# Attention of the first 256 queries four heads to a visit, two heads to a bank; last residual added on TensorE

## The chip, the cores and the metric

The kernel runs on one core of a Trainium2 chip. The metric is the device time of one launch in microseconds. The median of three runs of the kernel before is 459.55 us (459.14 to 460.91).

## What is computed

A decoder layer for 512 tokens of width 1024 in float32. One input projection feeds two causal token mixers, a gated recurrence (HGRN2) and a sparse attention, whose outputs are gated, projected, merged, projected once more and added to the input ahead of a layer norm. The parts that the change touches are these:

```python
def dsa_mix(q, k, v, q_idx, k_idx, w_idx, rel_bias):      # 8 heads of 64, blocks of 128 queries
        score = jnp.einsum('bth,bths->bts', wb * (IDX_HEADS ** -0.5), jax.nn.relu(dots))
        score = jnp.where(causal[None], score, -jnp.inf)
        _, idx = lax.top_k(score, topk)                   # 128 keys for each query, shared by all heads
        logits = jnp.einsum('bthd,btkhd->bhtk', qh, ks) * (HEAD_DIM_B ** -0.5)
        logits = logits + bias.transpose(0, 3, 1, 2)      # T5 bias of the distance
        p = jax.nn.softmax(logits, axis=-1)
        o = jnp.einsum('bhtk,btkhd->bthd', p.astype(vs.dtype), vs)
...
    merged = jax.nn.sigmoid(ga) * ua + jax.nn.sigmoid(gb) * ub
    y = jnp.einsum('bld,de->ble', merged, w_out)
    return layer_norm(ALPHA * x + y, ln_g, ln_b)
```

## The kernel before

**The stream.** Every large product is done in three matmuls of 512 columns on parts with a rounded high half and the rest as low half (`split_product`, L516 to L518). The weights come in 31 units of 256 columns (`UNITS`), then four of the output projection. A unit is four quarters of twelve such matmuls; a quarter has the number q = 4u + (0 to 3). Two PSUM banks take turns for the projections (`proj_bank`); bank i of unit u is filled in quarters 4u + 2i and 4u + 2i + 1, must be read by `leave_bank` and is filled again four quarters after it was begun. ScalarE rounds each unit's weights to `w_hi` (L842), and GpSimd (L1681), for units 17 to 24 VectorE (L1498), subtracts to get `w_lo`.

**Side work.** Behind each quarter TensorE runs `side(q)`, and ScalarE, VectorE and GpSimd have a `side(q)` of their own, in which the work of the same quarter stands in a fixed order. Every engine goes through its list in order and waits on semaphores; it may run ahead of or lag behind the others. Tables say what falls into which quarter.

**Attention.** The 32 items (`ITEMS`) are pairs of a block b of 128 queries and a head h: blocks 0 to 3 of heads 0 to 3 (items 0 to 15), then of heads 4 to 7 (16 to 31). An item has (b + 1) x 128 keys; keys outside the top k are not gathered but get a penalty. One item goes through these steps:

- GpSimd, `bias_and_penalty` (L1699, L1697): bias plus penalty into one of two `logit` buffers, that of item i once `logits` of item i - 2 has run.
- TensorE, `scores` (L652, L653): two matmuls into one of two banks (`log_bank`), in quarter `Q_ITEM[i]`.
- VectorE, `logits` (L1318): adds bank and buffer into `prob` (four buffers), negates, and takes the row's extreme.
- ScalarE, `softmax_exp` (L931); VectorE, `invert_sums` (L1329); ScalarE, `normalise` (L939).
- TensorE, `turn_probs` (L662): b + 1 turnings of 128 x 128 into one of two banks (`turn_bank`), two quarters after the scores.
- VectorE, `move_probs` (L1306): out of that bank into `prob_t`.
- TensorE, `attend` (L677): values times probabilities, two heads at a time, in quarter `Q_ATTEND[i]`; one quarter later VectorE gates the four heads (`gate_group`, L1340).

Items go two to a visit. Within a quarter TensorE does values, then turnings, then scores. VectorE does bank copies of the projection, `move_probs`, gating, `logits`, one round of the top k, sums, further rounds, then low parts and the steps of the recurrence. A round of the top k (L1294, L1295) takes the 8 largest of the remaining scores; the 16 rounds of the last query block are spread over quarters 38 to 48. ScalarE does bank copies, scalings of the quarter before (items 0 to 15), rounding of weights, exponentials, scalings of the same quarter (items 16 to 31), and then `forget`, the decay of the recurrence, that of the first two heads in quarters `Q_PREP[0]` to + 2 (64 to 66), of the others from `Q_PREP[1]`. Units 15 and 16 are the inputs of `forget`; `leave_bank` copies their banks to `cum` (L913).

**The end.** The output projection fills eight banks (`y_bank[half][t]`, four blocks of tokens, two halves of 512 columns), 24 matmuls each. For each, `residual` (L1546, L1548) adds ALPHA times the input (`x_res`) to the bank into `y_sb` and takes statistics. Behind the second half of a block VectorE joins them (L1653), centres (L1658), and scales (L1664), with the inverse deviation from ScalarE (L1178, L1180), and the two halves go out. Only the last block's second half has nothing of TensorE beside it.

## Time and profile before

| | us | share |
|---|---|---|
| median of 3 runs | 459.55 | |
| profiled execution | 459.29 | |
| its span | 457.5 | |
| TensorE busy | 449.4 | 98% |
| TensorE weight loads | 368.1 | 80% |
| VectorE busy | 292.3 | 64% |
| ScalarE busy | 223.1 | 49% |
| GpSimd busy | 163.3 | 36% |

The span runs from the first to the last instruction of the profiled execution; 1.8 us of its time lie around it. The granted clock of TensorE is 0.995 of its full 2.4 GHz over the span. Matmuls are pipelined: the time that a row gives for one is longer than the time by which it holds up the next, so their cost is read from start to start. VectorE's share is an average; from 46 to 137 us it is busy for nine tenths of the time and more.

### The profile page before, as it was taken

The page shows a single profiled execution, that of the slowest core. Times are in us where ns is not written, and L with a number is a line of the kernel's source. Part 1 is how long each engine was busy: PE and PEld are TensorE (multiplying, and loading weights), DVE is VectorE, ACT ScalarE, POOL GpSimd, SP SyncE. Part 2 cuts the span into 40 slices and gives each one's busy share as a digit, 9 for nine tenths or more (in the row PEclk, how much of TensorE's full clock was granted, in tenths as well). Part 3 has the DMA queues.
Part 4 walks back from the last instruction along what each step waited for, and adds up shares of the span by engine and source line. Part 5 has one row for each costly group of instructions (what it writes and reads, how often), then busy time and mean ns, then how long its engine had stood idle before and what let it go on. Part 6 is the DMA issues. An engine that isn't in the chain of part 4 may idle for free.

```text
span 457.5 us, 7667 instructions
## 1 busy us (share of the span) xinstructions
PE 449.4 (98%) x2970; PEld 368.1 (80%) x2970; DVE 292.3 (64%) x558; ACT 223.1 (49%) x378; POOL 163.3 (36%) x161
## 2 busy tenths in 40 slices
PE   9999999999999999999999999999999999999993
PEld 7778888888888788888888887887888888888882
DVE  4546589999999853346989994880643040662286
ACT  5735445253345746294877475735774415341000
POOL 0444432582259813581004000000064554984000
PEclk9999999999999999999999999999999999999998
DMA  8908122256023720204030222031044222374022
GB/s 251 304 15 293 73 82 93 92 152 217 0 93 92 186 92 1 93 1 149 36 95 1 95 93 93 1 122 66 1 123 153 93 92 93 119 257 176 0 92 92
DMA packets 17299, 47.73 MB, mean 104 GB/s; under 512 B 2504, under 2 KB 4336, under 8 KB 17264
## 3 DMA queue, kind: packets, MB, share of 16 engines
q1 hardware_dynamic: 17024, 47.05, 31.5%
q8 instruction: 23, 0.38, 0.3%
q10 hardware_dynamic: 240, 0.20, 0.1%
q14 instruction: 12, 0.10, 0.1%
HBM read 43.04 MB, written 2.11 MB: 99 GB/s over the span
## 4 chain that ended last, share of the span: by engine, by line
PE 98%; DVE 1%; DVEq 0%; issue 0%; POOL 0%; POOLq 0%
PE bank L516 27%; PE bank L517 26%; PE bank L518 26%; PE bank L677 2%; PE bank L662 2%; PE bank L713 2%; PE bank L760 2%; PE bank L653 1%; PE bank L652 1%; PE bank L804 1%; PE bank L642 1%; PE bank L641 1%; PE bank L559 1%; PE bank L560 1%; PE bank L564 1%; PE bank L746 1%
## 5 line engine op out<-in xcount | busy, mean ns | idle before, releaser
L1681 POOL TENSOR_TENSOR w_lo<-w_raw,w_hi 128x512 fp32r<-128x512 f32 x92 | 122.6, 1358 | 161.8 <-ACT w_hi L842 161.8
L516 PE MATMUL bank<-x_hi,w_hi 128*128 128x512 f32 x336 | 132.9, 396 | 0.0
L517 PE MATMUL bank<-x_lo,w_hi 128*128 128x512 f32 x336 | 131.1, 390 | 0.0
L518 PE MATMUL bank<-x_hi,w_lo 128*128 128x512 f32 x336 | 131.0, 390 | 0.0
L516 PEld LDWEIGHTS bank<-x_hi,w_hi 128*128 128x128 f32 x336 | 63.1, 188 | 13.9 <-issue 0.8
L518 PEld LDWEIGHTS bank<-x_hi,w_lo 128*128 128x128 f32 x336 | 63.1, 188 | 13.6
L517 PEld LDWEIGHTS bank<-x_lo,w_hi 128*128 128x128 f32 x336 | 63.1, 188 | 12.1
L842 ACT ACTIVATE w_hi<-w_raw 128x1024 fp32r<-128x1024 f32 (+2 forms) x67 | 66.5, 1014 | 10.1 <-PE bank L518 5.8
L931 ACT ACTIVATE prob<-prob,nmax 128x128 f32<-128x128 f32 (+3 forms) x32 | 17.7, 555 | 41.6 <-DVE nmax L1318 41.5
L1294 DVE MAX8 best<-score 128x8 f32<-128x256 f32 (+2 forms) x48 | 26.8, 559 | 1.1
L1306 DVE COPY prob_t<-bank 128x128 f32<-128x128 f32 (+3 forms) x32 | 14.3, 486 | 19.0 <-PE bank L662 18.9
L1295 DVE MATCH_REPLACE8 score<-best,score 128x256 f32<-128x256 f32 (+2 forms) x48 | 26.0, 542 | 0.0
L516 PE MATMUL bank<-w_hi,x_hi 128*128 128x512 f32 x64 | 25.3, 395 | 0.0
L518 PE MATMUL bank<-w_hi,x_lo 128*128 128x512 f32 x64 | 25.0, 390 | 0.0
L517 PE MATMUL bank<-w_lo,x_hi 128*128 128x512 f32 x64 | 24.9, 390 | 0.0
L516 PE MATMUL bank<-o_hi,w_hi 128*128 128x512 f32 x64 | 24.9, 389 | 0.0
L517 PE MATMUL bank<-o_lo,w_hi 128*128 128x512 f32 x64 | 24.9, 389 | 0.0
L518 PE MATMUL bank<-o_hi,w_lo 128*128 128x512 f32 x64 | 24.9, 389 | 0.0
L921 ACT ACTIVATE relus<-bank 128x256 f32<-128x256 f32 (+2 forms) x24 | 10.5, 489 | 21.0 <-PE bank L642 21.0
L1699 POOL TENSOR_TENSOR logit<-t,pen 128x256 f32<-128x256 f32 x24 | 17.4, 740 | 9.1 <-DVE nmax L1318 9.1
L1498 DVE TENSOR_TENSOR w_lo<-w_raw,w_hi 128x512 fp32r<-128x512 f32 x32 | 20.5, 683 | 0.0
L1284 DVE SCALAR_TENSOR_TENSOR score<-relus,w_idx,score 128x256 f32<-128x256 f32 (+2 forms) x21 | 15.7, 747 | 7.6 <-ACT relus L921 5.9
(206 smaller groups left out, 756.1 us busy)
## 6 DMA issues: line engine op xcount, KB each, us to landing
w_raw<-in_w_units SPq DMA_DIRECT2D x66, 512.0 KB, 4.7
out<-y_sb SPq DMA_DIRECT2D x8, 256.0 KB, 2.0
x_raw_hi<-in_x_t SPq DMA_DIRECT2D x4, 256.0 KB, 5.0
x_raw_lo<-in_x_t SPq DMA_DIRECT2D x4, 256.0 KB, 6.5
t_turned<-t_row SPq DMA_DIRECT2D x1, 1024.0 KB, 9.6
q_hi_g<-q_hi_g SPq DMA_DIRECT2D x8, 128.0 KB, 3.9
x_res_hi<-in_x_tok SPq DMA_DIRECT2D x2, 512.0 KB, 5.2
x_res_lo<-in_x_tok SPq DMA_DIRECT2D x2, 512.0 KB, 6.8
```

The lines of the kernel that those rows point to most:

```text
L516: nc.tensor.matmul(dst, a_hi, b_hi, start=first, stop=False)
L517: nc.tensor.matmul(dst, a_hi, b_lo, start=False, stop=False)
L518: return nc.tensor.matmul(dst, a_lo, b_hi, start=False, stop=last)
L842: nc.scalar.activation(split_target(u, kiwi_hi, x_hi, w_hi)[:, k, :], raw(u)[:, k, :], ACT.Copy).then_inc(done, 1)
L931: nc.scalar.activation(prob[:, i % 4, 0:n], prob[:, i % 4, 0:n], ACT.Exp, bias=nmax[:, i % 4:i % 4 + 1], scale=-1.0, accum_out=prob_sum[:, ...
L1284: ins = nc.vector.scalar_tensor_tensor(out=score[b][:], in0=relus[:, i % 2, 0:n], scalar=w, in1=score[b][:], op0=ALU.mult, op1=ALU.add)
L1294: link(nc.vector.max(best8[:], score[b][:]))
L1295: link(nc.vector.match_replace(score[b][:], best8[:], score[b][:], TAKEN))
L1306: nc.vector.tensor_copy(prob_t[:, i % 4, 0:n], turn_bank[i % 2][:, 0:n]).then_inc(turn_out[i % 2], 1)
L1498: nc.vector.tensor_tensor(split_target(u, kiwi_lo, x_lo, w_lo)[:, k, :], raw(u)[:, k, :], split_target(u, kiwi_hi, x_hi, w_hi)[:, k, :].bi ...
L1681: nc.gpsimd.tensor_tensor(split_target(u, kiwi_lo, x_lo, w_lo)[:, k, :], raw(u)[:, k, :], split_target(u, kiwi_hi, x_hi, w_hi)[:, k, :].bi ...
L1699: nc.gpsimd.tensor_tensor(logit[:, i % 2, n - band:n], t5[:, h, 2 * P - band:], pen[b][:, n - band:] if b else causal_sb[:], ALU.add).then ...
```

## The change

Items of blocks 0 and 1 go four to a visit. Heads 0 and 1 of such four fill the first part of the two score banks, heads 2 and 3 the columns behind it (`columns`, `shares_bank`); the same holds for the turned probabilities. VectorE waits until all four are there (`filled`). `Q_ITEM`, `Q_TURN` (new) and `Q_ATTEND` are written out. The list of quarters with scores, turnings or values becomes 39, 43, 47, 49, 51, 53, 55, 57, 59, 61, 63, 65, 67, 68; it was all odd quarters from 39 to 55 and all from 55 to 67. The last items are scored in quarter 65 for 64, turned in 67 for 66; the last values are in 68 for 67, and the second `forget` begins in 69 for 68.

The residual of the last half bank is no longer added by VectorE: ScalarE rounds ALPHA times the input to `ax_hi`, VectorE makes the rest `ax_lo`, and two matmuls with the rounded identity `id_r` put them into the bank ahead of the 24 others. Statistics and centring of this half read the bank.

```diff
--- before.py
+++ after.py
@@ -79,10 +79,12 @@
 LO_FROM = {19: 73}
 SLOTS = {8: 2, 9: 0, 10: 1, 11: 2, 12: 0, 13: 1, 14: 2, 17: 2}
 Q_DOTS = 4 * 3
-Q_ITEM = [39 + 2 * (i // 2) if i < 16 else 55 + 4 * ((i - 16) // 2) // 3 for i in range(len(ITEMS))]
-Q_ATTEND = [Q_ITEM[4 * (i // 4) + 3] + (4 if i < 16 else 3) for i in range(len(ITEMS))]
+Q_ITEM = [q for q, n in ((39, 4), (43, 4), (47, 2), (49, 2), (51, 2), (53, 2), (55, 4), (57, 4), (59, 2), (61, 2),
+                         (63, 2), (65, 2)) for _ in range(n)]
+Q_TURN = [q + (4 if i < 8 else 2) for i, q in enumerate(Q_ITEM)]
+Q_ATTEND = [q for q in (47, 49, 53, 57, 59, 61, 65, 68) for _ in range(4)]
 Q_GROUP = [Q_ATTEND[4 * n + 3] + 1 for n in range(len(GROUPS))]
-Q_PREP = (64, 68)
+Q_PREP = (64, 69)
 Q_NEAR = (72, 81)
 Q_TREE = (73, 83)
 TREE_AT = (1, 2, 2, 4, 4, 7, 7)
@@ -187,6 +189,8 @@
             o_hi, o_lo = (sb(n, [P, 8, SEQ], F32R, s) for n in ("o_hi", "o_lo"))
             m_hi, m_lo = (sb(n, [P, KT, SEQ], F32R, s) for n in ("m_hi", "m_lo"))
             g_b = sb("g_b", [P, 4, SEQ], stack=s)
+            with ExitStack() as s2:
+                ax_hi, ax_lo = (sb(n, [P, SEQ], F32R, s2) for n in ("ax_hi", "ax_lo"))
             mix = sb("mix", [P, 2, SEQ], stack=s)
@@ -209,6 +213,7 @@
         causal_sb = sb("causal_sb", [P, P])
         ones_sb = sb("ones_sb", [P, P])
         ones_r = sb("ones_r", [P, P], F32R)
+        id_r = sb("id_r", [P, P], F32R)
         masks_sb = sb("masks_sb", [P, (len(LEVELS) - 2) * 16 + 32], I32)
         att_d = sb("att_d", [P, 2, TB, 32])
         bias = sb("bias", [P, 2 * NMAIN])
...
@@ -366,6 +372,23 @@
 
         def items_at(q):
             return [i for i in range(len(ITEMS)) if Q_ITEM[i] == q]
+
+        def turns_at(q):
+            return [i for i in range(len(ITEMS)) if Q_TURN[i] == q]
+
+        def shares_bank(i):
+
+            return ITEMS[i][0] < 2
+
+        def columns(i):
+
+            n = (ITEMS[i][0] + 1) * P
+            first = i % 4 // 2 * n if shares_bank(i) else 0
+            return slice(first, first + n)
+
+        def filled(i):
+
+            return 4 * (i // 4) + 4 if shares_bank(i) else i + 1
 
         def attends_at(q):
             return [i for i in range(0, len(ITEMS), 2) if Q_ATTEND[i] == q]
@@ -644,22 +667,24 @@
 
             def scores(i):
                 b, h = ITEMS[i]
-                dst = log_slot(QK0 + i)
+                second = shares_bank(i) and i % 4 >= 2
+                dst = (log_bank[i % 2] if second else log_slot(QK0 + i))[:, columns(i)]
                 if b == 0 and h % 2 == 0:
                     pe.wait_ge(q_twice[h // 4][h // 2 % 2], 16 * 4)
                     wait_proj_out(pe, f"kb{h // 4}", h // 2 % 2)
                 n = (b + 1) * P
-                nc.tensor.matmul(dst[:, 0:n], q_hi(h)[:, queries(b)], k_hl(h)[:, 0:n], start=True, stop=False)
-                nc.tensor.matmul(dst[:, 0:n], q_lo(h)[:, queries(b)], k_hl(h)[:, 0:n],
+                nc.tensor.matmul(dst, q_hi(h)[:, queries(b)], k_hl(h)[:, 0:n], start=True, stop=False)
+                nc.tensor.matmul(dst, q_lo(h)[:, queries(b)], k_hl(h)[:, 0:n],
                                  start=False, stop=True).then_inc(log_full, 1)
 
             def turn_probs(i):
                 b, h = ITEMS[i]
                 pe.wait_ge(norm_done, i + 1)
-                if i >= 2:
+                if i >= 2 and not (shares_bank(i) and i % 4 >= 2):
                     wait_turn_out(pe, i - 2)
+                dst = turn_bank[i % 2][:, columns(i)]
                 for c in range(b + 1):
-                    mm = nc.tensor.transpose(turn_bank[i % 2][:, queries(c)], prob[:, i % 4, queries(c)], id_sb[:])
+                    mm = nc.tensor.transpose(dst[:, queries(c)], prob[:, i % 4, queries(c)], id_sb[:])
                 mm.then_inc(turn_full, 1)
 
             def attend(i):
@@ -781,7 +806,7 @@
                         dots(i)
                 for i in attends_at(q):
                     attend(i)
-                for i in items_at(q - 2):
+                for i in turns_at(q):
                     turn_probs(i)
                 for i in items_at(q):
                     scores(i)
@@ -824,6 +849,11 @@
                         pe.wait_ge(proj_out[t - 2], NPROJ[NMAIN])
                     else:
                         pe.wait_ge(up_out[t], 2 * KT // 4)
+                    last_bank = (half, t) == (1, TB - 1)
+                    if last_bank:
+                        pe.wait_ge(ax_lo_done, 1)
+                        nc.tensor.matmul(bank[:], id_r[:], ax_hi[:], start=True, stop=False)
+                        nc.tensor.matmul(bank[:], id_r[:], ax_lo[:], start=False, stop=False)
                     for k in range(KT):
                         if half == 0 and t == 0:
                             pe.wait_ge(m_lo_done, k + 1)
@@ -832,7 +862,8 @@
                             mm = split_product(bank[:], *m, x_hi[:, k, :], x_lo[:, k, :], k == 0, k == KT - 1)
                         else:
                             mm = split_product(bank[:].rearrange("p (s n) -> p s n", s=2), *m,
-                                               w_hi[:, 0:2, k, :], w_lo[:, 0:2, k, :], k == 0, k == KT - 1)
+                                               w_hi[:, 0:2, k, :], w_lo[:, 0:2, k, :],
+                                               k == 0 and not last_bank, k == KT - 1)
                     mm.then_inc(y_full, 1)
 
 
@@ -1127,6 +1158,7 @@
             act.wait_ge(pool_set, 1)
             nc.scalar.activation(ones_r[:], ones_sb[:], ACT.Copy).then_inc(ones_done, 1)
             act.wait_ge(early_in, 32)
+            nc.scalar.activation(id_r[:], id_sb[:], ACT.Copy).then_inc(ones_done, 1)
             for q in range(4 * NMAIN):
                 u, j = q // 4, q % 4
                 if j == 0 and u >= 1:
@@ -1173,6 +1205,9 @@
             nc.scalar.preload_act_table_set("natural_log_exp_and_others")
             split_hi(NMAIN + 3, 0)
             split_hi(NMAIN + 3, 1)
+            act.wait_ge(m_lo_done, KT)
+            act.wait_ge(res_in[TB - 1], 16)
+            nc.scalar.activation(ax_hi[:], x_res[1][:, 1, 512:], ACT.Copy, scale=ALPHA).then_inc(ax_hi_done, 1)
             for t in range(TB):
                 act.wait_ge(y_aggr, t + 1)
                 nc.scalar.activation(rstd[:, t, 0:1], aggr[:, t, 1:2], ACT.Ln, bias=eps[:, 1:2]).then_inc(ln_log, 1)
@@ -1299,23 +1334,23 @@
 
             def move_probs(i):
                 b, h = ITEMS[i]
-                dve.wait_ge(turn_full, i + 1)
+                dve.wait_ge(turn_full, filled(i))
                 if i >= 4:
                     dve.wait_ge(pv_done, i - 3)
                 n = (b + 1) * P
-                nc.vector.tensor_copy(prob_t[:, i % 4, 0:n], turn_bank[i % 2][:, 0:n]).then_inc(turn_out[i % 2], 1)
+                nc.vector.tensor_copy(prob_t[:, i % 4, 0:n], turn_bank[i % 2][:, columns(i)]).then_inc(turn_out[i % 2], 1)
 
             def logits(i):
 
                 b, h = ITEMS[i]
-                dve.wait_ge(log_full, QK0 + i + 1)
+                dve.wait_ge(log_full, QK0 + filled(i))
                 dve.wait_ge(logit_pre, i + 1)
                 if b >= 2:
                     dve.wait_ge(logit_far, FAR_COPIES[i])
                 if i >= 4:
                     dve.wait_ge(turn_full, i - 3)
                 n = (b + 1) * P
-                nc.vector.tensor_tensor_reduce(out=prob[:, i % 4, 0:n], in0=log_bank[i % 2][:, 0:n],
+                nc.vector.tensor_tensor_reduce(out=prob[:, i % 4, 0:n], in0=log_bank[i % 2][:, columns(i)],
                                                in1=logit[:, i % 2, 0:n], scale=-QSCALE, scalar=3e38,
                                                op0=ALU.add, op1=ALU.min,
                                                accum_out=nmax[:, i % 4:i % 4 + 1]).then_inc(log_out[i % 2], 1)
@@ -1538,6 +1573,13 @@
                 nc.vector.tensor_tensor(m_lo[:, m, :], mx, m_hi[:, m, :].bitcast(F32),
                                         ALU.subtract).then_inc(m_lo_done, 1)
 
+            def last_residual_lo():
+
+                dve.wait_ge(ax_hi_done, 1)
+                nc.vector.scalar_tensor_tensor(out=ax_lo[:], in0=x_res[1][:, 1, 512:], scalar=ALPHA,
+                                               in1=ax_hi[:].bitcast(F32), op0=ALU.mult,
+                                               op1=ALU.subtract).then_inc(ax_lo_done, 1)
+
             def residual(t, half):
 
                 c = slice(half * 512, half * 512 + 512)
@@ -1558,7 +1600,7 @@
                 for i in range(2 * (q - Q_DOTS), 2 * (q - Q_DOTS) + 2):
                     if 0 <= i < len(DOTS):
                         add_score(i)
-                for i in items_at(q - 2):
+                for i in turns_at(q):
                     move_probs(i)
                 for n in groups_at(q):
                     gate_group(n)
@@ -1646,8 +1688,14 @@
             merge(KT - 1)
             for t in range(TB):
                 residual(t, 0)
+                if t == 1:
+                    last_residual_lo()
             for t in range(TB):
-                residual(t, 1)
+                if t < TB - 1:
+                    residual(t, 1)
+                else:
+                    dve.wait_ge(y_full, 2 * TB)
+                    link(nc.vector.bn_stats(stats[:, t, 1, :], y_bank[1][t][:]))
                 if t == 0:
                     dve.wait_ge(ln_in, 32)
                 nc.vector.bn_aggr(aggr[:, t, :], stats[:, t, :, :].rearrange("p a b -> p (a b)")).then_inc(y_aggr, 1)
@@ -1655,7 +1703,8 @@
                 halves = slice(0, 512), slice(512, 1024)
                 for c in halves:
                     y = y_sb[:, t, c]
-                    centred = nc.vector.scalar_tensor_tensor(out=y, in0=y, scalar=aggr[:, t, 0:1], in1=ln_gb[:, 0, c],
+                    src = y_bank[1][t][:] if t == TB - 1 and c.start else y
+                    centred = nc.vector.scalar_tensor_tensor(out=y, in0=src, scalar=aggr[:, t, 0:1], in1=ln_gb[:, 0, c],
                                                              op0=ALU.subtract, op1=ALU.mult)
                 link(centred)
                 dve.wait_ge(ln_rstd, t + 1)
```

The order in which instructions stand moves as follows. On VectorE in quarter 43, from the last two copies of turned probabilities to the round of the top k; L1306 is `move_probs` (L1341 in the new file), L1318 is `logits` (L1353), L1294 and L1295 a round of the top k (L1329, L1330). Before:

```order
L1306 COPY prob_t<-bank4 128x128
L1306 COPY prob_t<-bank5 128x128
L1318 ISA prob,nmax<-bank2,logit 128x256
L1318 ISA nmax 128x1
L1318 ISA prob,nmax<-bank3,logit 128x256
L1318 ISA nmax 128x1
L1294 MAX best8<-score3 128x8
L1295 MATCH_REPLACE score3<-best8,score3 128x512
```

After:

```order
L1341 COPY prob_t<-bank4 128x128
L1341 COPY prob_t<-bank5 128x128
L1353 ISA prob,nmax<-bank2,logit 128x256
L1353 ISA nmax 128x1
L1353 ISA prob,nmax<-bank3,logit 128x256
L1353 ISA nmax 128x1
L1353 ISA prob,nmax<-bank2,logit 128x256
L1353 ISA nmax 128x1
L1353 ISA prob,nmax<-bank3,logit 128x256
L1353 ISA nmax 128x1
L1329 MAX best8<-score3 128x8
L1330 MATCH_REPLACE score3<-best8,score3 128x512
```

Two more copies stand ahead of these in the new order, and behind them stand four `logits` in place of two, and only then the round of the top k.

On ScalarE, from the first step of the first `forget` in quarter 64 to the copy of bank 0 in quarter 66; L951 to L962 are `forget`, L842 rounds weights, L913 is the bank copy. In the new file L962 and L970 are exponential and scaling, L982 to L993 `forget`, L873 rounds, L944 is the bank copy. Before:

```order
L931 ACTIVATE prob,prob_sum<-prob,nmax 128x512 x2
L939 ACTIVATE prob<-prob,prob_rcp 128x512 x2
L951 ACTIVATE lb<-lb 128x4
L952 ACTIVATE dec<-dec 128x1024
L954 ACTIVATE dec<-dec 128x1024
L842 ACTIVATE w_hi<-w_raw 128x1024
L956 ACTIVATE dec<-dec 128x1024
L962 ACTIVATE dec<-dec,lb 128x512 x2
L913 ACTIVATE cum<-bank0,bias 128x512
```

After:

```order
L982 ACTIVATE lb<-lb 128x4
L983 ACTIVATE dec<-dec 128x1024
L985 ACTIVATE dec<-dec 128x1024
L873 ACTIVATE w_hi<-w_raw 128x1024
L962 ACTIVATE prob,prob_sum<-prob,nmax 128x512 x2
L970 ACTIVATE prob<-prob,prob_rcp 128x512 x2
L987 ACTIVATE dec<-dec 128x1024
L993 ACTIVATE dec<-dec,lb 128x512 x2
L944 ACTIVATE cum<-bank0,bias 128x512
```

Exponentials and scalings of the last two items stand inside `forget` and no longer ahead of it.

On VectorE, the steps behind the last product of all; L1546 is the residual, L1548 its statistics (L1698 in the new file). Before:

```order
L1546 SCALAR_TENSOR_TENSOR y_sb<-x_res_lo,bank5 128x512
L1548 BN_STATS stats<-y_sb 128x6
L1653 BN_AGGR aggr<-stats 128x2
L1658 SCALAR_TENSOR_TENSOR y_sb<-y_sb,aggr,ln_gb 128x512 x2
L1664 SCALAR_TENSOR_TENSOR y_sb<-y_sb,rstd,ln_gb 128x512 x2
```

After:

```order
L1698 BN_STATS stats<-bank5 128x6
L1701 BN_AGGR aggr<-stats 128x2
L1707 SCALAR_TENSOR_TENSOR y_sb<-y_sb,aggr,ln_gb 128x512
L1707 SCALAR_TENSOR_TENSOR y_sb<-bank5,aggr,ln_gb 128x512
L1713 SCALAR_TENSOR_TENSOR y_sb<-y_sb,rstd,ln_gb 128x512 x2
```

The step of the residual is gone, and the statistics and the second centring read bank 5.

## Rows read from the trace of the kernel before

**Rows 1.** The page, its fourth part: shares of the chain that ended last, by engine.

```profile
PE 98%; DVE 1%; DVEq 0%; issue 0%; POOL 0%; POOLq 0%
```

**Rows 2.** Timeline of TensorE at quarter 39: start us, length us, instruction.

```profile
119.10 0.39 PE L518 MATMUL bank<-w_hi,x_lo 128*128 128x512 f32 x1
119.32 0.22 PE L652 MATMUL bank<-k_hl_g,q_hi_g 128*128 128x128 f32 x1
...
119.72 0.45 PE L516 MATMUL bank<-w_hi,x_hi 128*128 128x512 f32 x1
```

**Rows 3.** The same at quarters 58 and 66, two visits of turnings alone.

```profile
188.23 0.38 PE L662 MATMUL bank<-id_sb,prob 128*128 128x128 f32 x2
188.37 0.47 PE L516 MATMUL bank<-w_hi,x_hi 128*128 128x512 f32 x1
...
220.90 1.03 PE L662 MATMUL bank<-id_sb,prob 128*128 128x128 f32 x8
221.69 0.48 PE L516 MATMUL bank<-x_hi,w_hi 128*128 128x512 f32 x1
```

**Rows 4.** Groups of weight loads: count, busy us, mean ns, idle us before them.

```profile
L677 PEld LDWEIGHTS bank<-prob_t,v_b 128*64 128x64 f32 x160 | 8.6, 136 | 2.8 <-issue 2.8
```

**Rows 5.** Timelines of VectorE and GpSimd at quarters 39 and 43.

```profile
120.34 0.29 DVE L1318 CUSTOM_DVE_ANT_0 prob<-bank,logit 128x128 f32<-128x128 f32 x1
...
120.56 0.28 DVE L1318 CUSTOM_DVE_ANT_0 prob<-bank,logit 128x128 f32<-128x128 f32 x1
...
120.72 0.88 POOL L1699 TENSOR_TENSOR logit<-t,causal_sb 128x128 f32<-128x128 f32 x2 [14.50 <-DVE nmax L1318]
...
132.41 0.41 DVE L1318 CUSTOM_DVE_ANT_0 prob<-bank,logit 128x256 f32<-128x256 f32 x1
...
132.75 0.42 DVE L1318 CUSTOM_DVE_ANT_0 prob<-bank,logit 128x256 f32<-128x256 f32 x1
...
132.91 1.44 POOL L1699 TENSOR_TENSOR logit<-t,pen 128x256 f32<-128x256 f32 x2 [2.28 <-DVE nmax L1318]
```

**Rows 6.** Timeline of VectorE at quarter 45; in brackets idle time and its end.

```profile
138.73 0.76 DVE L1306 COPY prob_t<-bank 128x256 f32<-128x256 f32 x2 [0.46 <-PE bank L662]
```

**Rows 7.** Timelines from quarter 49 to 51: VectorE, ScalarE, TensorE.

```profile
154.38 1.02 DVE L1306 COPY prob_t<-bank 128x384 f32<-128x384 f32 x2
...
158.66 1.13 ACT L939 ACTIVATE prob<-prob,prob_rcp 128x384 f32<-128x384 f32 x2
...
159.33 1.05 PE L662 MATMUL bank<-id_sb,prob 128*128 128x128 f32 x6
```

**Rows 8.** Timelines from quarter 64 to 68: VectorE, ScalarE, TensorE.

```profile
214.23 0.69 DVE L1318 CUSTOM_DVE_ANT_0 prob<-bank,logit 128x512 f32<-128x512 f32 x1 [0.61 <-PE bank L653]
...
216.72 1.34 ACT L939 ACTIVATE prob<-prob,prob_rcp 128x512 f32<-128x512 f32 x2 [0.23 <-DVE prob_rcp L1329]
...
221.11 1.04 ACT L956 ACTIVATE dec<-dec 128x1024 f32<-128x1024 f32 x1
...
222.69 1.28 DVE L1306 COPY prob_t<-bank 128x512 f32<-128x512 f32 x2
...
223.48 0.67 ACT L913 ACTIVATE cum<-bank,bias 128x512 f32<-128x512 f32 x1
...
224.60 1.97 PE L677 MATMUL bank<-prob_t,v_b 128*64 128x128 f32 x32
...
225.74 2.34 DVE L1369 TENSOR_TENSOR_SCAN cum<-reset,k_c 128x512 f32<-128x512 f32 x2
```

**Rows 9.** Timelines of VectorE behind the last product, and of ScalarE near the start.

```profile
450.50 0.69 DVE L1546 SCALAR_TENSOR_TENSOR y_sb<-x_res_lo,bank 128x512 f32<-128x512 f32 x1 [0.88 <-PE bank L518]
451.22 0.69 DVE L1548 BATCH_NORM_STATS2 stats<-y_sb 128x6 f32<-128x512 f32 x1
...
19.80 0.68 ACT L880 ACTIVATE q_hl<-bank,bias 64x512 fp32r<-64x512 f32 x1 [1.18 <-PE bank L564]
```

**Rows 10.** Timeline of GpSimd at quarter 42.

```profile
129.34 1.29 POOL L1681 TENSOR_TENSOR w_lo<-w_raw,w_hi 128x512 fp32r<-128x512 f32 x1
```

1 line of the change is left out of this document (added).

## The prediction, made before the change was run

> **What bounds the kernel now.** I read the page first, and on it the chain of work that ended last: TensorE carries 98% of it, VectorE 1% [rows 1]. So a change pays in two ways only: TensorE gets less to do, or what comes after its last product gets shorter. It costs as soon as another engine is late for TensorE. I then read the timelines, one engine at a time, around the places that the change moves. I call twelve products of 512 columns a quarter. One starts 0.227 us after the other (119.10 to 119.32 [rows 2]), so a quarter is 2.72 us. Side work stands between quarters: I call that a visit, and number it by its quarter q.
>
> **TensorE's share of the attention: -0.1 us.** The count of matmuls stays: 80 turnings, 160 for the values, 64 for scores. What goes is the number of visits. What is one worth? Four score matmuls of one block hold the stream from 119.32 to 119.72, and with the 0.06 us that the first product behind them starts late, 0.46 us, 0.115 each [rows 2]. Two turnings take 0.14 us until the next product, eight take 0.79 [rows 3]: 0.108 each, and nothing fixed is left over for the visit itself. I add up the visits of quarters 39 to 68 from these pieces before and after: the difference is under 0.1 us. Merging visits is cost or gain of nothing. Value matmuls do have a start of their own, 2.8 us of idle time in all [rows 4], that is 0.35 before each of the eight visits with values; but there are eight such visits after the change as well.
>
> **Four heads to a visit on VectorE: +1.1 us.** VectorE takes scores out of the bank in `logits`, and each needs a term from GpSimd in one of two `logit` buffers, which that same `logits` frees. With two heads to a visit both buffers were filled long before. With four, the third and the fourth wait while VectorE stands, for its order is fixed. At quarter 39 the first `logits` starts at 120.34, the next 0.22 later; GpSimd starts 0.38 after the first and takes 0.88 for two, 0.44 each [rows 5]. So the third can start 0.88 after the first, not 0.44, and the fourth at 1.3, not 1.1: with the wait for all four score matmuls (0.06, since VectorE gets there only at 120.34 anyway) some 0.75 us. At quarter 43, 256 wide, VectorE's step is 0.34, GpSimd starts 0.50 after and takes 0.72 each [rows 5]: third at 1.27 for 0.68, fourth at 2.0 for 1.6, so 0.97 us. VectorE has almost no air here, because the rounds of the top k fill it: all I find idle up to quarter 48 is 0.46 us [rows 6] and a tenth. So 1.7 - 0.6 = 1.1 us of lag remain at quarter 49. Who waits for it? The turnings of quarter 51: already before, their probabilities are scaled in 1.13 us from 158.66, with TensorE at the turnings from 159.33; these six take 1.05 us from the start of the first to the end of the last, where five steps of 0.108 and a last one of 0.27 make 0.81 [rows 7]. So a quarter of a microsecond is lost there already, and nothing is left to hide in. This chain starts with VectorE's copies at 154.38 [rows 7] and goes late by 1.1 us, and TensorE with it. Bounds: nothing, if the lag is won back; 2.0 us, if none of the idle time is used and the copies of four heads in quarter 47 (0.7 us more than two) are added to it. I take 1.1, the sum of the rows.
>
> A rule of the Trainium skill speaks against sharing a bank: two engines may not be on one bank and quadrant at once ("PSUM — Partial Sum Buffer", PSUM bank collisions raise a hardware error). That is why VectorE now waits for all four heads. Taken alone, it would cost the 0.46 us of four more score matmuls; by the trace 0.06, since VectorE comes late anyway.
>
> **The last visits: +1.0 us.** Scores of the last two heads move from quarter 64 to 65, their turnings from 66 to 67, the last values from 67 to 68. On ScalarE, exponentials and scalings of these heads now stand between the two parts of `forget`, ahead of the copy of `cum` that frees bank 0 for quarter 68. From the same steps before: first `logits` at 214.23, scalings end at 216.72 + 1.34 = 218.06, 3.83 later; the rest of `forget` plus nothing else takes 223.48 - 221.11 = 2.37, the copy 0.67 [rows 8]: 6.9 us. The first `logits` starts about as the visit of quarter 65 ends (its copies of heads 4 and 5 go first). TensorE is back for the bank after two quarters and the 8 turnings of quarter 67, 5.44 + 0.87 = 6.3 us. Before, it had the 32 value matmuls in front of quarter 68, 1.97 us from 224.60 [rows 8], and about as much to spare. So it waits 0.5 us. Then VectorE: the copies of the last two turned heads (1.28 us, at 222.69 before) now stand behind two scans (2.34 us from 225.74 [rows 8]). These end about 4.9 us after the copy of `cum` begins; TensorE, 0.7 for that copy, 2.72 for quarter 68 and 1.0 for the values of heads 4 and 5, is there at 4.4. It waits another 0.5 us. Bounds: 0 to 2.0 (once more the same, if `forget` starts no earlier than before; its first part can now start before the scores of quarter 65, since nothing but bank copies is ahead).
>
> **The rest of the second group: 0.** Here VectorE has idle time. Four heads scored at quarter 57 must be scaled by quarter 59: with 2.0 us to the fourth `logits` as at quarter 43 [rows 5], then the last exponential, the sums and four scalings of somewhat under the 0.57 us that one of 384 columns takes [rows 7], I get about 5 us, against 5.44 plus 0.7 of values in front of the turnings. If that is a little longer, TensorE waits at 59.
>
> **The last residual: -0.27 us.** One step of VectorE behind the last product goes, 451.22 - 450.50 = 0.72 us [rows 9]; two products of 0.227 come ahead, 0.45 on TensorE. The rounding and its rest are one step each of ScalarE and VectorE in a stretch where both only wait for TensorE's banks. The statistics and one centring now read the bank; a read of the bank at 450.50 takes the 0.69 us that a read of memory takes at 451.22 [rows 9], so nothing is added. The rounding of the identity is 128 columns wide; it falls into ScalarE's idle 1.18 us before 19.80, where a step of 512 columns takes 0.68 [rows 9]; without that cover it would delay the first banks, and TensorE at quarter 8, by its own length.
>
> The Trainium skill says otherwise for the bank reads: VectorE pays 120 cycles instead of 58 for a source in PSUM ("VectorE: DVE Perf Modes", The TRN2 errata), an estimate of 0.065 us each, which would leave -0.14 us. The rows show no such difference.
>
> **Sum.** -0.1 + 1.1 + 1.0 - 0.27 = +1.7. The profiled execution took 459.29 us (span 457.5), the median of three is 459.55: I add to 459.29 and get 461.0.
>
> **Rivals.** (a) *All waits are covered.* VectorE's lag is absorbed and the last visits fit: 459.29 - 0.37 = 458.9. For it: both waits are small against quarters of 2.72 us. Against it: TensorE already waits at 160 before. (b) *Slower: GpSimd comes to the third head with weights in front.* At quarter 43 the terms of heads 2 and 3 stand behind the four low parts of weight unit 11 on GpSimd, which wait for ScalarE's rounding, and that now stands behind four scalings. I expect them done at 131, 2.5 us ahead; if they aren't by 133.6, one more piece of 1.29 us [rows 10] goes on the lag: 461.0 + 1.3 = 462.3. (c) *Each visit has a fixed price.* If the 0.35 us ahead of values (2.8 over 8 [rows 4]) were every visit's, six to seven fewer would give -2.3, and with the tail 456.7. [Rows 3] speak against it. (d) *The change does less than it says*: the two products cost as much as the step they replace; then 461.3, same as the forecast.
>
> **Chances.** Forecast with (d) 0.56, (a) 0.20, (b) 0.20, (c) 0.04. The range that leaves out no more than 0.2 runs from (a) 458.9 to the upper bounds, 462.8. A measurement of this kernel tells 0.5%, 2.3 us, from no change: slower means over 461.8, which is (b) and a tenth of the forecast, 0.28; faster is (c), 0.04; same 0.68.
>
> **What the new profile would show.** TensorE's turnings at quarter 51 with an idle time or a long group before them; VectorE idle between second and third `logits` at quarters 39 and 43, released by GpSimd; the copy of `cum` from bank 0 as releaser of the first product of quarter 68, and VectorE's copies as that of the last values; a tail from the last product 0.72 us shorter. If the visits sum to less than before by over half a microsecond, the price per matmul was wrong; if VectorE's copies at 49 are no later against TensorE, the lag was; if the last tail is not shorter, the bank reads were.

## The result, and the profile after the change

| | before | after |
|---|---|---|
| median | 459.62 us (459.05 to 460.91, 10 runs) | 461.50 us (461.31 to 463.24, 10 runs) |
| ratio, 95% interval | | 1.0050 (1.0042 to 1.0059) |
| span of the profiled execution | 457.5 us | 459.5 us |

The change costs 1.9 us by the medians, 0.4 to 0.6% by the interval, which is clear of no change and brackets the 0.5% that the prediction took for the least that can be told. The time is half a microsecond over the forecast of 461.0. First the view that answers to [rows 1]: the page of the changed kernel, its first part and its chain of waits.

```profile
PE 449.8 (98%) x2972; PEld 368.3 (80%) x2972; DVE 292.8 (64%) x558; ACT 224.1 (49%) x380; POOL 162.5 (35%) x161
...
PE 61%; DVE 6%; issue 2%; ACT 1%; POOL 0%; DVEq 0%
```

TensorE is as busy as before. The 61% for 98% must not be read as a share lost to other engines: the shares add up to 70%, since the chain is followed back no further than this step of VectorE, 132.63 us into the span of 459.5.

```profile
132.63 0.33 DVE prob L1353
```

From there to 159.63 us, the turnings of quarter 51, the chain runs over VectorE, GpSimd and ScalarE; behind that it is TensorE's nearly throughout. Who ended TensorE's waits, the list of them says (us in total, times, longest). In the kernel before it holds one row, the same as the first here (under L804).

```profile
PE bank L829 <- POOL eps L1721: 1.1, 1, 1.1
PE bank L738 <- issue: 0.9, 1, 0.9
PE bank L687 <- ACT prob L970: 0.7, 1, 0.7
PE bank L539 <- ACT cum L944: 0.4, 1, 0.4
PE bank L702 <- DVE prob_t L1341: 0.3, 1, 0.3
```

L687 is `turn_probs`, L702 `attend`, L539 to L541 are `split_product`; L738 is the product of the recurrence's tree (`tree`). Three of the four new waits are those of the prediction, the largest is not. The list leaves out a fifth, smaller loss, at the first product of quarter 46. VectorE, then TensorE:

```profile
136.64 0.67 DVE L1290 TENSOR_TENSOR v_b<-bank,bias_vb 128x512 f32<-128x512 f32 x1
```
```profile
137.01 0.39 PE L541 MATMUL bank<-x_hi,w_lo 128*128 128x512 f32 x1
137.37 0.50 PE L539 MATMUL bank<-x_hi,w_hi 128*128 128x512 f32 x1
137.70 0.39 PE L540 MATMUL bank<-x_lo,w_hi 128*128 128x512 f32 x1
```

Products follow each other at 0.2265 us, and these two steps take 0.69: 0.24 us are lost, 0.26 over quarters 45 and 46 together. VectorE's copy out of a projection bank ends at 137.31, just ahead of the late product. In the kernel before it began at 134.69, over three microseconds ahead of TensorE's return.

To add up what a visit costs I take its extra time: from the start of the last product ahead of it to the start of the third behind it, less three steps of 0.2265 us. The rows for quarter 51 after the change, from TensorE's timeline:

```profile
158.55 0.39 PE L541 MATMUL bank<-x_hi,w_lo 128*128 128x512 f32 x1
159.63 1.05 PE L687 MATMUL bank<-id_sb,prob 128*128 128x128 f32 x6 [0.69 <-ACT prob L970]
...
161.90 0.39 PE L541 MATMUL bank<-w_hi,x_lo 128*128 128x512 f32 x1
```

161.90 - 158.55 - 0.68 = 2.67 us, against 1.90 before. This measure repeats to 0.02 us from profile to profile, far better than the times do. All kernels of this study (each is explained with its experiment below), by groups of visits (where the last scores are in quarter 64, the turnings of quarter 65 are in the third column, as they are in the same visit as the last scores elsewhere):

| kernel | 39 to 51 | 53 to the last scores | last turnings and values | 77 | last residual's products | start of quarter 8 |
|---|---|---|---|---|---|---|
| before | 9.12 | 18.69 | 3.00 | 1.48 | 0 | 22.25 |
| after | 9.88 | 18.55 | 4.20 | 2.52 | 0.45 | 21.54 |
| own_terms | 8.77 | 18.55 | 4.19 | 2.50 | 0.45 | 22.40 |
| old_last | 9.84 | 18.53 | 3.00 | 3.02 | 0.45 | 22.26 |
| pad_after | 9.89 | 18.55 | 4.20 | 1.46 | 0.45 | 22.63 |
| tail_only | 9.11 | 18.69 | 3.00 | 1.47 | 0.45 | 22.58 |
| old_first | 9.12 | 18.55 | 4.21 | 1.46 | 0.45 | 22.20 |
| pad_before | 9.11 | 18.69 | 3.00 | 1.47 | 0 | 22.02 |
| early_step | 9.88 | 18.55 | 3.73 | 1.75 | 0.45 | 22.15 |
| scans_late | 9.88 | 18.55 | 3.63 | 2.28 | 0.45 | 22.51 |
| pad_238 | 9.12 | 18.69 | 3.00 | 2.59 | 0 | 22.10 |
| pad_256 | 9.88 | 18.55 | 4.21 | 2.35 | 0.45 | 22.84 |
| mend_pad | 8.77 | 18.53 | 3.00 | 1.46 | 0.45 | 22.45 |
| all_mended | 8.77 | 18.55 | 3.00 | 1.46 | 0.45 | 22.12 |

All other visits are equal to 0.04 us each. The last column is when TensorE begins the first product of quarter 8, in us. The table holds only what is lost at visits. Within the quarters the kernels agree to 0.05 us but for two places: the 0.26 us around the start of quarter 46, which only the changed kernel and the five others that keep its hand-off of four heads in the first group lose (0.26 to 0.31), and 0.14 us in quarter 72, in the kernel before, tail_only, pad_before and pad_238 alone, for which no run shows a cause.

From before to after: +0.76 - 0.14 + 1.20 + 1.04 + 0.45 = 3.3 us, less 0.72 at the tail, is +2.6; with +0.26 and -0.14 within the quarters +2.7; the opening, 0.71 shorter in this profile, makes it +2.0, and the spans differ by 2.0.

The opening is no part of the change: the ten other kernels with the change's edits to ScalarE's start begin quarter 8 at 22.12 us or later. In these two profiles it goes with the landing of the first piece of x, by ScalarE's first rounding after the change and before it:

```profile
3.92 0.63 ACT L891 ACTIVATE x_hi<-x_raw_hi 128x512 fp32r<-128x512 f32 x1 [1.91 <-DMA x_raw_hi<-in_x_t]
```
```profile
4.58 0.63 ACT L860 ACTIVATE x_hi<-x_raw_hi 128x512 fp32r<-128x512 f32 x1 [2.56 <-DMA x_raw_hi<-in_x_t]
```

That landing alone does not decide it: old_first and old_last round at 3.95 and 3.99 us and begin quarter 8 at 22.20 and 22.26. Over the fourteen profiles the rounding starts between 3.92 and 4.80 us, and quarter 8 between 21.54 and 22.84, in no order that follows the edits. So a median of five or ten executions is good to about half a microsecond here, and I lean on the extra times where a few tenths decide.

**The hand-off.** VectorE at quarters 39 and 43, the rows that answer to [rows 5]:

```profile
119.92 0.29 DVE L1353 CUSTOM_DVE_ANT_0 prob<-bank,logit 128x128 f32<-128x128 f32 x1
...
120.68 0.29 DVE L1353 CUSTOM_DVE_ANT_0 prob<-bank,logit 128x128 f32<-128x128 f32 x1 [0.47 <-POOL logit L1748]
...
133.92 0.43 DVE L1353 CUSTOM_DVE_ANT_0 prob<-bank,logit 128x256 f32<-128x256 f32 x1 [0.61 <-issue]
...
134.62 0.42 DVE L1353 CUSTOM_DVE_ANT_0 prob<-bank,logit 128x256 f32<-128x256 f32 x1 [0.27 <-issue]
```

With 0.12 us more at the fourth head of quarter 39 and 0.13 in front of its first, VectorE stands 1.60 us in quarters 39 to 47, for 0.46 before. Its copies of quarter 49 start at 154.69, for 154.38 [rows 7]; since TensorE had run 0.77 us ahead of its old times at quarter 39, that is 1.08 us late.

**The last visits.** ScalarE, TensorE, VectorE, TensorE again, the rows that answer to [rows 8]:

```profile
224.32 0.67 ACT L944 ACTIVATE cum<-bank,bias 128x512 f32<-128x512 f32 x1
```
```profile
225.04 0.50 PE L539 MATMUL bank<-x_hi,w_hi 128*128 128x512 f32 x1 [0.36 <-ACT cum L944]
```
```profile
228.03 1.26 DVE L1341 COPY prob_t<-bank 128x512 f32<-128x512 f32 x2
```
```profile
229.44 1.09 PE L702 MATMUL bank<-prob_t,v_b 128*64 128x128 f32 x16 [0.34 <-DVE prob_t L1341]
```

By extra times the first wait costs 1.52 - 0.89 = 0.63 us, the second 2.68 - 2.11 = 0.57. That is more than their rows give, 0.36 and 0.34: a row counts idle time from the end of the matmul ahead, and without a wait the next product starts some 0.24 us before that end (221.69 for 220.90 + 1.03 in [rows 3]).

**The tail.** VectorE behind the last product, answering to [rows 9]:

```profile
453.18 0.70 DVE L1698 BATCH_NORM_STATS2 stats<-bank 128x6 f32<-128x512 f32 x1 [1.33 <-PE bank L541]
453.91 0.21 DVE L1701 BATCH_NORM_AGGREGATE aggr<-stats 128x2 f32<-128x12 f32 x1
...
454.82 0.75 DVE L1707 SCALAR_TENSOR_TENSOR y_sb<-bank,aggr,ln_gb 128x512 f32<-128x512 f32 x1
455.60 1.42 DVE L1713 SCALAR_TENSOR_TENSOR y_sb<-y_sb,rstd,ln_gb 128x512 f32<-128x512 f32 x2
```

The last of VectorE's steps, the two scalings, in the kernel before:

```profile
453.64 1.42 DVE L1664 SCALAR_TENSOR_TENSOR y_sb<-y_sb,rstd,ln_gb 128x512 f32<-128x512 f32 x2
```

From VectorE's first step behind the last product (450.50 in [rows 9]) to its last end it took 455.06 - 450.50 = 4.56 us, and now takes 457.02 - 453.18 = 3.84.

**The unforeseen wait.** TensorE and VectorE in quarter 77:

```profile
258.19 1.27 PE L738 MATMUL bank<-q_c,k_c 128*32 128x16 f32 x123
...
259.05 0.69 DVE L1467 TENSOR_TENSOR q_c<-dec,q_a 128x512 f32<-128x512 f32 x1 [1.36 <-PE bank L738]
...
260.32 0.24 PE L738 MATMUL bank<-q_c,k_c 128*32 128x16 f32 x5 [0.85 <-issue]
```

In the kernel before, the same 128 matmuls run through in 1.34 us from 257.02. TensorE stops five matmuls ahead of the end of a group that has no wait inside it, and "issue" names no releaser. But the view of DMA traffic, cut to 257.8 to 258.1 us, shows one packet of a queue that carries instructions:

```profile
q8 instruction: 1, 0.02, 19.5%
```

In the kernel before, this queue has nothing between 256.9 and 258.3 us; the piece ahead of quarter 77 was fetched at 252.73. The packets hold 16 KB, and there is one for about each 256 instructions that TensorE runs. The Trainium skill says that an instruction takes 64 bytes ("Perfetto Trace Analysis", The 4-stage abstract model); with that 16 KB are 256 of them, and the trace agrees (240 to 270 from one fetch to the next where the stream is even).

### The profile page after: what moved, and what is told of

The parts are those of the page before. It is cut to its first block, busy times and chain, and to the rows that moved or that the text cites. A ratio compares the mean times of both kernels' runs of the same rounds, so it can differ in the third digit from the quotient of the medians.

```text
span 459.5 us, 7666 instructions
## 1 busy us (share of the span) xinstructions
PE 449.8 (98%) x2972; PEld 368.3 (80%) x2972; DVE 292.8 (64%) x558; ACT 224.1 (49%) x380; POOL 162.5 (35%) x161
## 3 DMA queue, kind: packets, MB, share of 16 engines
HBM read 43.04 MB, written 2.11 MB: 98 GB/s over the span
## 4 chain that ended last, share of the span: by engine, by line
PE 61%; DVE 6%; issue 2%; ACT 1%; POOL 0%; DVEq 0%
PE bank L539 17%; PE bank L541 17%; PE bank L540 17%; PE bank L738 2%; PE bank L785 2%; PE bank L702 2%; PE bank L687 1%; DVE score L1330 1%; DVE best L1329 1%; PE bank L771 1%; DVE prob_t L1341 1%; PE bank L677 1%; DVE q_lo_g L1281 1%; PE bank L676 1%; ACT prob L962 1%
## 5 line engine op out<-in xcount | busy, mean ns | idle before, releaser
L539 PE MATMUL bank<-x_hi,w_hi 128*128 128x512 f32 x336 | 132.7, 395 | 0.4 <-ACT cum L944 0.4
L541 PE MATMUL bank<-x_hi,w_lo 128*128 128x512 f32 x336 | 130.9, 390 | 0.0
L539 PEld LDWEIGHTS bank<-x_hi,w_hi 128*128 128x128 f32 x336 | 63.1, 188 | 14.6 <-issue 0.8
L541 PEld LDWEIGHTS bank<-x_hi,w_lo 128*128 128x128 f32 x336 | 63.1, 188 | 13.5
L873 ACT ACTIVATE w_hi<-w_raw 128x1024 fp32r<-128x1024 f32 (+2 forms) x67 | 66.4, 1014 | 10.2 <-PE bank L541 5.8
L962 ACT ACTIVATE prob<-prob,nmax 128x128 f32<-128x128 f32 (+3 forms) x32 | 17.8, 558 | 43.2 <-DVE nmax L1353 42.9
L1329 DVE MAX8 best<-score 128x8 f32<-128x256 f32 (+2 forms) x48 | 26.8, 559 | 1.1
L1341 DVE COPY prob_t<-bank 128x128 f32<-128x128 f32 (+3 forms) x32 | 13.9, 484 | 21.2 <-PE bank L687 21.1
L1330 DVE MATCH_REPLACE8 score<-best,score 128x256 f32<-128x256 f32 (+2 forms) x48 | 26.1, 543 | 0.0
L539 PE MATMUL bank<-w_hi,x_hi 128*128 128x512 f32 x64 | 25.1, 392 | 0.0
L541 PE MATMUL bank<-w_hi,x_lo 128*128 128x512 f32 x64 | 24.9, 390 | 0.0
L539 PE MATMUL bank<-o_hi,w_hi 128*128 128x512 f32 x64 | 24.9, 389 | 0.0
L541 PE MATMUL bank<-o_hi,w_lo 128*128 128x512 f32 x64 | 24.9, 389 | 0.0
```

Source lines behind the costliest of these rows:

```text
L539: nc.tensor.matmul(dst, a_hi, b_hi, start=first, stop=False)
L541: return nc.tensor.matmul(dst, a_lo, b_hi, start=False, stop=last)
L873: nc.scalar.activation(split_target(u, kiwi_hi, x_hi, w_hi)[:, k, :], raw(u)[:, k, :], ACT.Copy).then_inc(done, 1)
L962: nc.scalar.activation(prob[:, i % 4, 0:n], prob[:, i % 4, 0:n], ACT.Exp, bias=nmax[:, i % 4:i % 4 + 1], scale=-1.0, accum_out=prob_sum[:, ...
L1329: link(nc.vector.max(best8[:], score[b][:]))
L1330: link(nc.vector.match_replace(score[b][:], best8[:], score[b][:], TAKEN))
```

## The experiments

Each kernel was timed side by side with the kernel before, on the same chip; "before" stands for its median there.

**1. Is it GpSimd's hand-off?** `own_terms`: the third and fourth head's terms get columns of their own in the two `logit` buffers.

```diff
-                if i >= 2:
-                    wait_log_out(pool, QK0 + i - 2)
+                back = 4 if shares_bank(i) and i % 4 >= 2 else 2
+                if i >= back:
+                    wait_log_out(pool, QK0 + i - back)
...
-                nc.gpsimd.tensor_tensor(logit[:, i % 2, n - band:n],
+                nc.gpsimd.tensor_tensor(logit[:, i % 2, at + n - band:at + n],
...
-                                               in1=logit[:, i % 2, 0:n],
+                                               in1=logit[:, i % 2, columns(i)],
```

> The changed kernel, but GpSimd writes the terms of the third and fourth head of a four-head visit into columns of their own of the two logit buffers, so that it needn't wait for VectorE's first two steps. Theory (GpSimd's hand-off is the lag): VectorE's idle time between the second and third logits of quarters 39 and 43 (0.47 + 0.12 and 0.61 + 0.27 us after the change) goes, its copies in quarter 49 start over a microsecond earlier against TensorE, and TensorE's wait of 0.7 us at the turnings of quarter 51 goes: 461.5 - 0.8 = 460.7 us. Rival (the wait for all four score matmuls and the two more copies ahead of quarter 49 make the lag): VectorE's idle time moves by no more than 0.3 us, the wait at quarter 51 stays above 0.5 us, 461.3 to 461.5 us.

Measured: 460.65 us, before 459.45; ratio 1.0021 (1.0011 to 1.0031). VectorE's timeline at quarter 39 and in quarter 49:

```profile
120.76 0.29 DVE L1353 CUSTOM_DVE_ANT_0 prob<-bank,logit 128x128 f32<-128x128 f32 x1
...
120.97 0.29 DVE L1353 CUSTOM_DVE_ANT_0 prob<-bank,logit 128x128 f32<-128x128 f32 x1
...
153.91 1.01 DVE L1341 COPY prob_t<-bank 128x384 f32<-128x384 f32 x2
```

The third head follows the second without a gap, at quarter 43 too, and the copies of quarter 49 begin 0.78 us earlier although this execution began 0.86 later. The wait at quarter 51 is gone, and more: the visit takes 1.59 us, for 2.67 after and 1.90 before. So the kernel before lost 0.31 us there. The 0.26 us at the start of quarter 46 are gone too: the copy that they waited for begins 0.76 us earlier (135.88), on a clock 0.86 later. The rival falls: the two more copies and the wait for all four score matmuls stay in this kernel, and cost TensorE nothing.

**2. Are the two late waits those of the moved visits?** `old_last`: the last two heads in quarters 64, 66, 67 again.

```diff
-                         (63, 2), (65, 2)) for _ in range(n)]
+                         (63, 2), (64, 2)) for _ in range(n)]
-Q_ATTEND = [q for q in (47, 49, 53, 57, 59, 61, 65, 68) for _ in range(4)]
+Q_ATTEND = [q for q in (47, 49, 53, 57, 59, 61, 65, 67) for _ in range(4)]
-Q_PREP = (64, 69)
+Q_PREP = (64, 68)
```

> The changed kernel with the last visits where they were: the last two heads scored in quarter 64, turned in 66, their values in 67, the second forget from 68. Theory (ScalarE's copy of cum and VectorE's copies are late because of that move): TensorE's waits at quarters 67 and 68 go, 0.63 + 0.57 = 1.2 us by the extra time of these two visits. For the wait of 0.85 us inside the products of quarter 77 two theories differ: if it comes from the second forget, a quarter later, it goes too: 461.5 - 1.2 - 1.0 = 459.3 us; if it is TensorE's supply of instructions, it depends on how many instructions stand ahead, and may stay: 460.3 us, or go. Rival to all: a wait of the same size shows up at quarters 65 to 67 instead, since VectorE has six copies and the first part of forget there: 461.3 us.

Measured: 461.82 us, before 459.45; ratio 1.0047 (1.0034 to 1.0059). TensorE's waits:

```profile
PE bank L738 <- issue: 1.4, 1, 1.4
PE bank L829 <- POOL eps L1721: 1.1, 1, 1.1
PE bank L687 <- ACT prob L970: 0.7, 1, 0.7
```

The two waits are gone (3.00 us for 4.20), and none took their place in quarters 65 to 67. The time did not fall to the expected 460.3 us, since the wait in quarter 77 grew by half a microsecond, and the opening was 0.7 us longer than in the profile after. The second forget is back at quarter 68 here, so it isn't the cause of the wait in 77.

**3. The supply of instructions.** `pad_after` adds 48 instructions to TensorE's stream far ahead; `pad_256` adds 256; `pad_before` and `pad_238` add 216 and 238 to the kernel before. Both waits are on semaphores set long ago.

```diff
+            pads = [48]
+
+            def pad():
+
+                if pads[0]:
+                    pads[0] -= 1
+                    pe.wait_ge(pool_set, 1)
+                    pe.wait_ge(x_hi_done, KT)
+
             def split_product(dst, a_hi, a_lo, b_hi, b_lo, first, last):
                 nc.tensor.matmul(dst, a_hi, b_hi, start=first, stop=False)
+                pad()
                 nc.tensor.matmul(dst, a_hi, b_lo, start=False, stop=False)
+                pad()
```

> The changed kernel with 48 waits on long-set semaphores added to TensorE's stream, one between the products of each of its first 48, so that everything behind stands 48 instructions later; nothing else differs. TensorE's program comes in pieces of 16 KB, one for some 256 instructions; in the changed kernel one starts to be fetched at 257.88 us, at the beginning of the dense products of quarter 77, and TensorE stands for 0.85 us, released by nothing that the profile shows, near their end. Theory (supply of instructions): with the fetch 48 instructions earlier against the work, about 5 us, the wait goes: 461.5 - 0.9 = 460.6 us; the waits at quarters 51, 67 and 68 stay. Rival (TensorE waits for data of the products of quarter 77, later than before since the second forget is): the wait stays, 461.5 us or a tenth more.

Measured: 461.37 us, before 459.45; ratio 1.0039 (1.0027 to 1.0052). The list of waits has the three others and nothing at L738's place; the visit of quarter 77 takes 1.46 us for 2.52, and the piece was fetched 4.9 us ahead of it. The wait went as expected. The time did not go down by it: this profile's opening is 1.09 us longer than that of the profile after, as much as the visit won.

> The kernel before with 216 waits on long-set semaphores added to TensorE's stream, one after each of the first products; nothing else differs. In the kernel before the piece of TensorE's program ahead of quarter 77 is fetched about 36 instructions ahead of its dense products; 216 instructions more, with 256 to a piece, put the fetch of the piece behind to the start of these products, as in the changed kernel. Theory (supply of instructions): TensorE now stands 0.8 to 1.4 us inside the products of quarter 77, with no releaser: 459.45 + 1.0 = 460.5 us. Rival (the wait in the changed kernel comes from late data): no wait, 459.45 us or a tenth more.

Measured: 459.49 us, before 459.37; ratio 1.0003 (0.9994 to 1.0012); no wait. My arithmetic had missed the place. The fetch began 0.29 us after the start of the visit (at 257.08 us), but the piece ended only behind it. Where, the next run tells: there the end falls right behind the dense products, so 22 instructions fewer, eleven products with their loads, put it here at about 260.5 us, 3.4 us after the fetch. By itself this run looks like the rival's. It shows that a fetch at the start of the dense products is not enough. The next one has 22 instructions more:

> The kernel before with 238 instead of 216 waits on long-set semaphores added to TensorE's stream. With 216 the next piece of TensorE's program was fetched 0.3 us after the start of the dense products of quarter 77, and its end came only behind them. Theory (supply of instructions): 22 instructions more bring the end of the piece into these products, a few instructions before their last, as in the changed kernel, so that TensorE stands 0.6 to 1.4 us there with no releaser and goes on 2.2 to 2.4 us after the fetch has begun: 459.4 + 1.0 = 460.4 us. Rival (late data): no wait, 459.5 us.

Measured: 461.12 us, before 459.51; ratio 1.0036 (1.0022 to 1.005). TensorE's timeline at quarter 77:

```profile
256.88 1.32 PE L724 MATMUL bank<-q_c,k_c 128*32 128x16 f32 x128
259.37 0.39 PE L525 MATMUL bank<-x_hi,w_hi 128*128 128x512 f32 x1 [1.16 <-issue]
```

The kernel before, with nothing but waits on set semaphores added, has the wait, 1.16 us with no releaser, on the very first product behind the dense ones, where I had expected it a few instructions earlier. 22 instructions decide over it. The profiled execution took 460.34 us, as forecast; the median of the six is 0.8 over that, and what the others lost no profile shows.

> The changed kernel with 256 instead of 48 waits on long-set semaphores added to TensorE's stream. If a piece of its program holds 256 instructions, every border between two pieces falls where it fell without the additions. Theory (supply of instructions): the wait in quarter 77 that 48 additions took away is back, at the same product as in the changed kernel (248 instructions into that visit), 0.6 to 1.4 us long: 461.4 us. Rival (anything added ahead takes it away, by time and not by place): no wait, 460.5 us.

Measured: 462.10 us, before 459.51; ratio 1.0056 (1.0044 to 1.0068). TensorE's timeline:

```profile
259.43 1.27 PE L749 MATMUL bank<-q_c,k_c 128*32 128x16 f32 x123
261.40 0.24 PE L749 MATMUL bank<-q_c,k_c 128*32 128x16 f32 x5 [0.69 <-issue]
```

The wait is back at the same matmul, behind 123 of the 128. What 48 additions took away, 256 restore, at the same place: adding instructions is not what removes it. (The time is 0.7 us over the 461.4 expected; this profile's opening is 1.3 us longer than that of the profile after.) In all seven profiles with this wait TensorE goes on 2.15 to 2.44 us after the fetch has begun (257.88 to 260.32 after the change; 259.11 to 261.40 here), so the length of the wait is this less what the dense products still had to do. The Trainium skill gives a DMA a fixed cost of about 2.0 us beside its bytes, most of it until the last byte is confirmed ("DMA: Bandwidth & Descriptors", Anatomy of one DMA); for another path than this queue's, and the trace is near it.

The place alone does not make the wait. With 256 instructions to a piece, pad_238 says where the piece ends in the kernel before: 256 instructions into the group with 238 more ahead, so some 238 to 240 into it without them, and eight further on, at 246 to 248, in the changed kernel, which is where that one stops (123 matmuls with their loads). So the piece ends inside the dense products before the change too, and with 48 additions as well, at about 200. What those two have and the changed kernel has not is an early fetch: 4.3 and 4.9 us ahead of the group, for 0.3. Eight instructions fewer ahead moved the fetch from 36 recorded instructions ahead of the group to its start. Why it begins so much later, no run here shows.

**4. The two late waits apart.** `early_step`: on ScalarE one step of `forget` ahead of the last exponentials.

```diff
+                if q == Q_PREP[0] + 1:
+                    forget(0, 2)
                 for i in items_at(q):
                     softmax_exp(i)
```

> The changed kernel, but on ScalarE in quarter 65 the first step of the second part of forget (1.04 us) stands ahead of the exponentials of the last two heads, in whose place ScalarE waits 0.72 us for VectorE's logits. Theory (the copy of cum is late because exponentials and scalings stand ahead of the rest of forget): the copy starts 0.6 to 0.7 us earlier and TensorE's wait at the first product of quarter 68 (0.36 us in the profile, 0.63 with what the visit loses around it) goes; the last copies of VectorE come some 0.5 us earlier, TensorE 0.6 earlier, so its wait in the values of quarter 68 stays: 461.5 - 0.55 = 460.95 us. Rival (the wait is the bank's own, since the units follow too closely behind each other there): the copy is no earlier and the wait stays, 461.5 us.

Measured: 461.37 us, before 459.37; ratio 1.0048 (1.0035 to 1.006). ScalarE, then TensorE:

```profile
223.90 0.67 ACT L944 ACTIVATE cum<-bank,bias 128x512 f32<-128x512 f32 x1
```
```profile
225.04 0.48 PE L539 MATMUL bank<-x_hi,w_hi 128*128 128x512 f32 x1
...
229.55 1.09 PE L702 MATMUL bank<-prob_t,v_b 128*64 128x128 f32 x16 [0.50 <-DVE prob_t L1344]
```

The copy comes 0.42 us earlier on a clock that started 0.6 later, and quarter 68 begins without a wait (0.89 us for 1.52). The other wait stays and grows by 0.16, so the two visits gain 0.47 us.

`scans_late`: on VectorE the last part of the first `forget` one quarter later.

```diff
-                    if q in (Q_PREP[p], Q_PREP[p] + 1, Q_PREP[p] + 2):
+                    if q in (Q_PREP[p], Q_PREP[p] + 1):
                         forget(p, q - Q_PREP[p])
+                    if q == Q_PREP[p] + (3, 2)[p]:
+                        forget(p, 2)
```

> The changed kernel, but on VectorE the last part of the first forget (one addition and two scans, 3.6 us) stands in quarter 67, behind the copies of the last two turned heads, and no longer in quarter 66, ahead of them. Theory (those copies are late because of the scans): they start at about 224.7 instead of 228.0 us, TensorE's wait in the values of quarter 68 (0.34 us, 0.57 by the visit's extra time) goes, the one at the first product of quarter 68 stays: 461.5 - 0.57 = 460.95 us. Rival (the second forget or the low parts, which the scans now delay, make TensorE wait later): as much is lost behind quarter 68, 461.5 us or more.

Measured: 462.35 us, before 459.37; ratio 1.0063 (1.005 to 1.0075). VectorE, then TensorE:

```profile
225.28 1.29 DVE L1341 COPY prob_t<-bank 128x512 f32<-128x512 f32 x2 [0.29 <-PE bank L687]
...
229.54 2.34 DVE L1404 TENSOR_TENSOR_SCAN cum<-reset,k_c 128x512 f32<-128x512 f32 x2
```
```profile
226.05 0.50 PE L539 MATMUL bank<-x_hi,w_hi 128*128 128x512 f32 x1 [0.37 <-ACT cum L944]
...
229.00 1.97 PE L702 MATMUL bank<-prob_t,v_b 128*64 128x128 f32 x32
```

The values run through (2.11 us for 2.68), the wait at the first product stays, and nothing behind quarter 68 is longer. So each wait has the cause that the prediction gave it. The times of these two kernels did not fall with their visits, and both missed the 460.95 us expected: by the extra times and the losses within quarters, early_step should be 1.5 us over before and scans_late 1.9; their medians of five are 2.0 and 3.0 over. Of scans_late some 0.3 is a longer opening; the rest is open.

**5. Each half of the change alone.** `tail_only`: the kernel before with the last residual on TensorE, as in the diff of the change.

> The kernel before with the last residual on TensorE and nothing else of the change. Theory: 0.72 us less behind the last product, two products of 0.227 us more ahead of it: 459.6 - 0.27 = 459.35 us. Rival (bank reads cost VectorE more than reads of memory, or the two products stall on ax_lo): 459.6 us or more, with the statistics behind the last product longer than 0.7 us. The start: the changed kernel's first rounding of x began 0.66 us earlier than that of the kernel before (3.92 for 4.58 us); if the rounding of the identity or the buffers of the last residual make that, it shows here too, and the time is 458.7 us.

Measured: 459.24 us, before 459.45; ratio 0.9993 (0.9985 to 1.0002). Its profile has the two products' 0.45 us, no wait of TensorE, and the tail without the step. The first rounding of x begins at 4.80 us, so the short opening after the change wasn't the change's. The expected -0.27 lies within the interval, as does nothing at all.

`old_first`: the changed kernel with items 0 to 15 as before.

```diff
-Q_ITEM = [q for q, n in ((39, 4), (43, 4), (47, 2), (49, 2), (51, 2), (53, 2),
+Q_ITEM = [q for q, n in ((39, 2), (41, 2), (43, 2), (45, 2), (47, 2), (49, 2), (51, 2), (53, 2),
-Q_TURN = [q + (4 if i < 8 else 2) for i, q in enumerate(Q_ITEM)]
+Q_TURN = [q + 2 for q in Q_ITEM]
-Q_ATTEND = [q for q in (47, 49, 53, 57, 59, 61, 65, 68) for _ in range(4)]
+Q_ATTEND = [q for q in (45, 49, 53, 57, 59, 61, 65, 68) for _ in range(4)]
-                return ITEMS[i][0] < 2
+                return ITEMS[i][0] < 2 and i >= 16
```

> The changed kernel with the first group of heads (items 0 to 15) as before: two heads to a visit, a bank for each, quarters 39 to 57 as they were; second group, last visits and last residual stay changed. Theory (the four-head visits of the first group lose 0.8 us at quarter 51 and gain nothing elsewhere): the visits of quarters 39 to 51 take 9.1 us over their products for 9.9, the waits at 67 and 68 stay: 461.5 - 0.75 = 460.75 us, if the wait of TensorE in quarter 77 stays, and 1.05 less if the other count of instructions ahead of it takes that away. Rival (fewer visits are worth something that the extra times don't show): no faster than 461.5 us.

Measured: 460.32 us, before 459.37; ratio 1.0026 (1.0016 to 1.0035). The visits of quarters 39 to 51 are back at 9.12 us, the two late waits stay at 4.21, and the wait in quarter 77 is gone: four instructions more ahead of it, and the fetch began 4.8 us ahead of the visit instead of 0.3. The extra times give +0.78 us over before, the medians +0.95.

**6. All causes away.** `mend_pad` is `own_terms` with the last visits of `old_last` and 48 additions; `all_mended` keeps the change's own quarters and is `own_terms`, `early_step`, `scans_late` and 48 additions in one.

> The changed kernel with all that the runs so far say: columns of their own for the terms of the third and fourth head, the last visits where they were before, and 48 waits added ahead. Theory (the four waits of TensorE are all that the change costs; visits have no price of their own): no wait of TensorE from quarter 39 on, the extra times of the visits of quarters 39 to 68 sum to 30.3 us (30.8 before, with 0.3 of waits at quarter 51 that go, and 0.16 for fewer visits), the tail is 0.72 us shorter for two products of 0.227: 459.4 - 0.3 - 0.16 - 0.27 = 458.7 us. Rival (taking waits away shows the next one, on VectorE or ScalarE): waits of more than 0.3 us elsewhere, 459.2 us or more.

Measured: 458.43 us, before 459.51; ratio 0.9974 (0.9963 to 0.9985).

> The changed kernel with its own quarters for the last visits, but with the four causes taken away: columns of their own for the terms, one step of forget ahead of the last exponentials on ScalarE, the last part of the first forget behind the last copies on VectorE, and 48 waits added ahead. Theory: early_step and scans_late each took away one of the two waits at quarters 67 and 68, together both: the visits sum to 30.2 to 30.4 us as with the old last visits, 458.7 us. Rival (what VectorE does later now makes TensorE wait behind quarter 68 once its other waits are gone): 459.3 us or more.

Measured: 458.35 us, before 459.51; ratio 0.9973 (0.9964 to 0.9983). TensorE's waits in this kernel:

```profile
PE bank L840 <- POOL eps L1737: 1.1, 1, 1.1
```

Neither has a wait of TensorE in its list behind the start, nor the loss at quarter 46, and both are faster than either kernel, by 1.1 us than before and by about 3 than after. Their visits of quarters 39 to 68 sum to 30.3 us, the same with the merged last visits and without.

## Why the prediction was right, and where

**TensorE's share, -0.1.** Right. Without its waits the changed kernel's visits of quarters 39 to 68 sum to 32.63 - 0.77 - 0.63 - 0.57 = 30.66, for 30.81 before. mend_pad and all_mended say it again from the other side: their sums fall by 0.5, and 0.31 of that is an old wait. The pieces were right too: eight score matmuls of 128 columns take 0.92 us for twice 0.46, and eight turnings 0.87. Rival (c), a fixed price for a visit, is gone.

**Four heads on VectorE, +1.1.** The mechanism was right, and so was the size, but TensorE paid at two places and not at one. Idle time of VectorE: 1.7 us forecast, 1.60 found (at quarter 39 0.75 forecast and 0.72 found, at 43 0.97 and 0.88); lag at its copies of quarter 49: 1.1 and 1.08. TensorE, forecast to pay it all at quarter 51, paid 0.77 there and 0.26 before, at the start of quarter 46, where the late VectorE had yet to copy the projection's bank; that wait the prediction had not, and own_terms takes it away with the other. By it TensorE comes some 0.24 us later to quarter 49, which leaves 0.84 of the 1.08; 0.77 + 0.26 = 1.03 in all. The sum also hides things that cancel. VectorE stood 0.13 us ahead of the first `logits` for its full bank, where I had 0.06. Its reads of a row's extreme, 0.08 us each, run beside the next step where there is no wait and stood alone at four of these. And its last step of the top k took 1.03 us for 1.36:

```profile
152.99 1.36 DVE L1297 TENSOR_SCALAR pen<-score 128x512 f32<-128x512 f32 x1
```
```profile
153.74 1.03 DVE L1332 TENSOR_SCALAR pen<-score 128x512 f32<-128x512 f32 x1
```

It takes 1.02 to 1.05 us in every kernel with the first group's four-head visits and 1.35 to 1.37 in every one without; what in them makes it shorter, no run here separates.

**The last visits, +1.0.** Right, and in size: 0.63 and 0.57 for 0.5 and 0.5, each with the releaser that was named, and each taken away by moving what the prediction had put in its way.

**The rest of the second group, 0.** Right: 18.55 us for 18.69, no wait at quarter 59.

**The last residual, -0.27.** Right by the rows: the tail is 0.72 us shorter, the two products take 0.45. Statistics read the bank in 0.70 us and memory in 0.69, no more. The Trainium skill has VectorE pay 120 cycles for 58 with a source in PSUM ("VectorE: DVE Perf Modes", The TRN2 errata), by an estimate 0.065 us a step; the trace does not agree. By time alone it can't be told from nothing.

**Rivals.** (a), all waits covered, fell with three waits. Of (b), GpSimd was done with its low parts at 130.4, where 131 was forecast, 2.6 us ahead of the third head. Its number, 462.3, is nearer to the outcome than (a)'s, but not by its mechanism. (Two small slips in the working change nothing: by [rows 5] the third head can start 0.82 us after the first, not 0.88, and 0.20 with a tenth of 0.56 is a chance of 0.26, not 0.28.)

**What the prediction had not.** A fifth term of +1.04: a piece of TensorE's program ends in the dense products of quarter 77, and the next is fetched only as they begin. No step of the sum failed for it; the sum was short of a term. Nothing in the list of edits points there, since no instruction of that visit changed; what changed in TensorE's list is that eight fewer recorded instructions stand ahead of it (3017 for 3025). With it the sum is -0.16 + 0.77 + 0.26 + 1.20 + 1.04 - 0.27 = 2.8, less the 0.14 of quarter 72 is 2.7 on 459.3, or 462.0. pad_256, a twin of the changed kernel with the same ends of pieces and the same four waits, came out at +2.6 over before. The changed kernel itself came out at +1.9, and its profile shows an opening 0.7 us shorter than before. Seven of its ten executions, the profiled one among them, lie within 0.3 us of each other, so they may share it; their openings were not recorded, and that stays open. So the forecast of 461.0 was good within its range partly because something that it lacked was halved by something that no forecast could hold.

## What to carry to other kernels

When work of several heads is merged into one visit, count the buffers at each hand-off, not only those that the change speaks of: here a third and fourth head shared banks well, and waited for the two small buffers of a third engine. Before moving a step later, list what stands behind it on each engine up to the next bank that TensorE wants back; both late waits followed from rows that were there before. And where dense groups of small matmuls stand in the stream, an edit far ahead can cost or give a microsecond by where the pieces of the program end and when the next is fetched, so read the instruction packets of the profile before an effect is put down to the edit.

## What the runs showed of the hardware

TensorE's program comes in packets of 16 KB while it runs, some 256 instructions each. At the pace of the large products a packet lasts 26 to 29 us and none of its fetches shows. A group of 128 small matmuls and their loads uses up 256 instructions in 1.3 us. Where a piece ended near its end or just behind it and the next was fetched from 0.85 us ahead of the group to 0.46 us into it (seven kernels), TensorE stood until 2.15 to 2.44 us after the fetch had begun, with 0.09 to 1.36 us of idle time, which cost 0.28 to 1.55 us of its stream; the profile calls it "issue". The same group with the fetch 4 to 5 us ahead (before, pad_after, tail_only, old_first, mend_pad, all_mended) has no such wait, though by the count of instructions the piece ends inside it there too, and neither has pad_before, where the piece ends some eleven products behind the group.
